# Closing the two seams of a two-block transformer kernel: squares kept apart and added at the end on VectorE, the second panel's matmuls one chunk behind, the third panel split inside the opening

## The reference, cut to what matters

```python
for l in range(DEPTH):                       # first block, DEPTH = 2
    h = rms_norm(x, pre_norm_g[l])
    proj = h @ w_in[l]
    ...
    y = jnp.concatenate([ya, yb], axis=-1) @ w_out[l]
    x = x + rms_norm(y, post_norm_g[l])
...
h = jnp.concatenate([meta, x, ...], axis=1)  # second block
hn = rmsnorm(h, norm_mix[0])
p = hn @ w_in
```

## Time and profile before

| | |
|---|---|
| median of three runs | 2347.67 us (2346.99 to 2349.81) |
| the profiled execution's own time | 2351.86 us |
| its span, first to last instruction | 2350.1 us |
| PE busy | 2241.6 us, 95% of the span |
| DVE, ACT, POOL busy | 1120.9, 971.2, 640.3 us (48%, 41%, 27%) |
| mean granted clock of TensorE | 0.977 of full speed |
| first seam | from about 352 us on |
| second seam | from about 685 us on |

### The profile page before, as it was taken

The page is one execution under the profiler, slowest core; times in us unless marked ns, Lnnn a source line. Parts: engine busy times, 40 slices in busy tenths (PEclk is TensorE's granted clock), DMA queues, the critical chain, the costliest instruction groups (busy, mean ns, idle before and its releaser), DMA issues. The chain is left out here.

```text
span 2350.1 us, 35450 instructions
## 1 busy us (share of the span) xinstructions
PE 2241.6 (95%) x14814; PEld 1988.4 (85%) x14814; DVE 1120.9 (48%) x1665; ACT 971.2 (41%) x1410; POOL 640.3 (27%) x498
## 2 busy tenths in 40 slices
PE   7998999998999999898999999999999989999998
PEld 5886568886579988896799999999898979988987
DVE  2457535657542224795544434444555444443443
ACT  5345643356533325425523313334555533322332
POOL 2112321113222514327223302322333312320321
PEclk9999999999999999997999999999999999999999
DMA  5341023210122211221133333323111113324322
GB/s 187 123 148 47 0 72 100 90 55 5 36 78 73 73 64 41 65 61 70 41 98 90 85 90 103 85 78 98 39 55 37 36 54 91 90 75 114 90 80 73
DMA packets 235215, 175.64 MB, mean 75 GB/s; under 512 B 7732, under 2 KB 230060, under 8 KB 234544
## 3 DMA queue, kind: packets, MB, share of 16 engines
q1 hardware_dynamic: 235056, 173.37, 24.7%
HBM read 171.20 MB, written 10.09 MB: 77 GB/s over the span
## 5 line engine op out<-in xcount | busy, mean ns | idle before, releaser
L331 DVE TENSOR_TENSOR panel_lo<-panel_raw,panel_hi 128x2048 fp32r<-128x2048 f32 (+2 forms) x148 | 325.9, 2202 | 278.1 <-ACT panel_hi L323 278.1
L323 ACT ACTIVATE panel_hi<-panel_raw 128x2048 fp32r<-128x2048 f32 (+2 forms) x151 | 268.4, 1777 | 366.7 <-PE product L429 256.7
L429 PE MATMUL product<-scaled_hi,panel_hi 128*128 128x272 f32 (+2 forms) x1232 | 282.4, 299 | 2.6 <-PEq L485 1.4
L429 PE MATMUL product<-scaled_lo,panel_hi 128*128 128x272 f32 (+2 forms) x1232 | 283.0, 299 | 0.0
L429 PE MATMUL product<-scaled_hi,panel_lo 128*128 128x272 f32 (+2 forms) x1232 | 282.7, 299 | 0.0
L429 PEld LDWEIGHTS product<-scaled_hi,panel_hi 128*128 128x128 f32 x1232 | 196.5, 188 | 11.8 <-issue 3.0
L429 PEld LDWEIGHTS product<-scaled_hi,panel_lo 128*128 128x128 f32 x1232 | 195.4, 188 | 7.4
L429 PEld LDWEIGHTS product<-scaled_lo,panel_hi 128*128 128x128 f32 x1232 | 194.5, 188 | 6.7
L442 PE MATMUL product_banks<-panel_hi,scaled_hi 128*128 128x256 f32 x696 | 195.4, 281 | 3.2 <-DVE panel_lo L331 3.2
L442 PE MATMUL product_banks<-panel_lo,scaled_hi 128*128 128x256 f32 x696 | 195.4, 281 | 0.0
L442 PE MATMUL product_banks<-panel_hi,scaled_lo 128*128 128x256 f32 x696 | 195.3, 281 | 0.0
(11 more groups left out here) (564 smaller groups left out, 5443.0 us busy)
## 6 DMA issues: line engine op xcount, KB each, us to landing
panel_raw<-in_w_in_dram SPq DMA_DIRECT2D x26, 1024.0 KB, 5.4
panel_raw<-in_ffn_w_gate_dram SPq DMA_DIRECT2D x44, 512.0 KB, 4.0
panel_raw<-in_ffn_w_up_dram SPq DMA_DIRECT2D x44, 512.0 KB, 5.3
panel_raw<-in_ffn_w_down_dram SPq DMA_DIRECT2D x32, 704.0 KB, 4.7
panel_raw<-in_even_w_in_dram SPq DMA_DIRECT2D x21, 1024.0 KB, 5.2
panel_raw<-in_odd_w_in_dram SPq DMA_DIRECT2D x12, 1024.0 KB, 5.2
panel_raw<-in_w_out_dram SPq DMA_DIRECT2D x8, 1024.0 KB, 6.8
panel_raw<-in_even_w_out_dram SPq DMA_DIRECT2D x8, 768.0 KB, 4.9
```

What stands on the lines that cost most here:

```text
L323: act.activation(c.hi[g % 2][:, 0:used], c.raw[g % 2][:, 0:used], ACT.Copy).then_inc(c.hi_made.sem, 1)
L331: dve.tensor_tensor(c.lo[g % 2][:, 0:used], c.raw[g % 2][:, 0:used], c.hi[g % 2][:, 0:used].bitcast(F32), ALU.subtract).then_inc(c.lo_made ...
L429: done = pe.matmul(banks[b], weight(w, k), a[:, k, u:v], start=(k == 0 and x == 0), stop=(k == chunks - 1 and x == 2))
```

## The change

It applies to both seams and to nothing else.

1. ACT's squares no longer go through two buffers. Chunk k of the squares is written over chunk k of `update.mix`, which is not needed any more once `hT` has been updated. The 16 meta tokens of the second seam, which are not part of `mix`, are squared ahead of it into a small tile (`extra_squares`).
2. POOL adds nothing any more. After the last chunk DVE adds the eight chunks as a tree of three instructions (2048, 1024 and 512 columns), with three small ones for the 16 meta tokens. PE then sums one total; the second matmul for the last square is gone.
3. PE does chunk k of the first panel's tiles together with chunk k - 1 of the second panel's. The sums stand ahead of the second panel's last chunk in the first seam, and behind it in the second seam (where they stood ahead of the tail tile).
4. The third panel is split inside the opening: on ACT after the last square (first seam) or after the roots (second seam), on DVE after the tree.

```diff
@@ led_product_stage
                 for k in range(KD):
                     if update is not None:
                         update.wait(act, k)
                     parts.act_hi(act, k)
                     if update is not None and k:
-                        norm.act_square(act, k - 1)
+                        norm.act_tree_square(act, k - 1)
                 if update is not None:
-                    norm.act_square(act, KD - 1)
+                    norm.act_tree_square(act, KD - 1)
+                    if wide:
+                        panels.hi(act, first + 2)
...
                 norm.act_inverse(act, sums, columns)
+                if update is not None and not wide:
+                    panels.hi(act, first + 2)
                 act.wait_ge(c.rstd_ready.sem, c.rstd_ready.at(norm.roots))
                 for g in range(first, first + n_panels):
...
-                    if first < g < last_split:
+                    if split_ahead <= g < last_split:
                         panels.hi(act, g + 1)
...
-                dve.wait_ge(c.rstd_ready.sem, c.rstd_ready.at(1))
+                if update is not None:
+                    norm.dve_tree(dve)
+                    panels.lo(dve, first + 2)
+                dve.wait_ge(c.rstd_ready.sem, c.rstd_ready.at(norm.roots))
...
-                if not summed:
-                    for k in range(norm.adds):
+                if not summed and update is None:
+                    for k in range(KD):
                         norm.pool_add(pool, k)
...
+                    in_first = panels.tiles_before(first + 1) - tile_0
+                    head, behind = ([at for at in opening if (at < in_first) == early] for early in (True, False))
+                    for k in range(KD + 1):
+                        if k < KD:
+                            parts.wait(pe, k)
+                            for at in head:
+                                done = chunk(at, k)
+                                if k == KD - 1:
+                                    done.then_inc(c.product_ready.sem, 1)
+                        if k == KD:
+                            if in_first - 1 not in head:
+                                whole_tile(in_first - 1)
+                            if wide:
                                 norm.pe_sums(pe, sums, columns)
+                        if k:
+                            for at in behind:
+                                done = chunk(at, k - 1)
+                                if k == KD:
+                                    done.then_inc(c.product_ready.sem, 1)
+                    if not wide:
+                        norm.pe_sums(pe, sums, columns)
@@ Rstd
+    def act_tree_square(self, act, k):
+        act.activation(self.tree[:, k, :], self.src(k)[:, self.extra:self.tokens], ACT.Square).then_inc(self.c.squared.sem, 1)
+
+    def dve_tree(self, dve):
...
+        each = 2 if extra else 1
+        dve.wait_ge(c.squared.sem, c.squared.at(KD + each - 1))
+        for n, half in enumerate((4, 2, 1)):
+            if n:
+                dve.wait_ge(c.paired.sem, c.paired.at(each * n))
+            a, b = self.tree[:, 0:half, :], self.tree[:, half:2 * half, :]
+            out = a if half > 1 else self.total[:, extra:self.tokens].rearrange("p (k n) -> p k n", k=1)
+            dve.tensor_tensor(out, a, b, ALU.add).then_inc(c.paired.sem, 1)
```

More of the change, by code:

```diff
@@ L234, in open_core @@
     c.x_added = count("x_added")
+    c.paired = count("paired")
     c.inner_made = count("inner_made")
@@ L621, in led_product_stage @@
                     spread=wide if spread is None else spread, side=None if held is None else "right", summed=summed, held=held,
-                    last_on_pe=wide and update is not None)
+                    tree=update.mix if update is not None else None)
         parts = Parts(c, stage if held is None else held, src, tokens, gain, room=whole, side=None if held is None else "right")
@@ L630, in led_product_stage @@
         sums, columns = (free[:, 0:tokens], free[:, 1016:1024]) if own else (psum[SUMS][:, 0, :], psum[COLUMNS][:, 0, 504:512])
+        split_ahead = first + (1 if update is None else 2)
         opening = () if update is None else (0, 1, 2, 3, 4, 5) if wide else (0, 1, 2, 3, 5, 6)
@@ L670, in _ @@
                     panels.hi(act, first)
+                if update is not None:
+                    norm.act_extra(act)
                 for k in range(KD):
@@ L3599, in __init__ @@
     def __init__(self, c, stage, src, tokens, squares=None, total=None, whole=False, columns=True, spread=True, last_on_pe=False,
-                 shape=lambda square: square, side=None, summed=False, held=None):
-        self.summed = summed
+                 shape=lambda square: square, side=None, summed=False, held=None, tree=None):
+        self.summed, self.tree = summed, tree
+        self.extra = tokens - SEQ if tree is not None else 0
+        if tree is not None:
+            squares, total = [], tree[:, 0, :] if total is None else total
+            self.extra_squares = c.sb("extra_squares", [P, KD, self.extra], into=stage) if self.extra else None
         self.c, self.src, self.tokens, self.last_on_pe, self.shape, self.columns = c, src, tokens, last_on_pe, shape, columns
@@ L3605, in __init__ @@
         self.adds = KD - 1 if last_on_pe else KD
-        self.staged = columns and last_on_pe
+        self.staged = tree is not None and spread is not False
         self.roots = 2 if self.staged else 1
-        self.squares = squares or [c.sb(f"squares{j}", [P, tokens], into=stage)[:] for j in range(2)]
+        self.squares = squares if squares is not None else [c.sb(f"squares{j}", [P, tokens], into=stage)[:] for j in range(2)]
         self.total = c.sb("square_total", [P, self.tiles * P if whole else tokens], into=stage)[:] if total is None else total
@@ L3632, in pe_sums @@
         for n, (square, start, stop) in enumerate(parts):
-            if n == 0:
+            if self.tree is not None:
+                pe.wait_ge(c.paired.sem, c.paired.at(6 if self.extra else 3))
+            elif n == 0:
                 pe.wait_ge(c.sum_added.sem, c.sum_added.at(0 if self.summed else self.adds))
@@ L3666, in close @@
         c = self.c
-        squares = () if self.summed else ((c.squared, KD), (c.sum_added, self.adds))
+        if self.tree is not None:
+            squares = ((c.squared, KD + (1 if self.extra else 0)), (c.paired, 6 if self.extra else 3))
+        else:
+            squares = () if self.summed else ((c.squared, KD), (c.sum_added, self.adds))
         for counter, n in (*squares, (c.sums_ready, self.roots), (c.root_made, self.roots), (c.rstd_ready, self.roots)):
```

21 lines of the change are left out of this document (10 added, 11 removed).

## The result

The kernel after took 2330.49 us (median of four runs, 2327.90 to 2331.72) against 2347.33 of before (four runs): ratio 0.9923, interval 0.9909 to 0.9936, or 16.8 us less. The forecast was 2335.9, the range 2332.5 to 2340.5. The sign and both seams came as forecast; 5 us more went than the sum had. A second series of the same kernel, further down, took 2335.99. Two single runs further down, 7602.7 us of before and 2476.35 of the kernel with the third panel late, lie far from all others of their kernels and are left out.

The account below looks back on a forecast made before the run. PE, busy 95% of 2350.1 us, was taken as the bound, with waits and slow stretches in both seams. Gains of 8.1 and 3.7 us, 11.8 in all, off the median 2347.67 gave 2335.9 us, range 2332.5 to 2340.5.

Parts of the forecast that it names:

- the sum: Both seams together: 8.1 us off the first and 3.7 off the second, 11.8 us in all, kept to the end.
- POOL slows DVE, and without it the period is 2.15: First seam: without POOL's additions, DVE's addition to `hT` returns from 1.79 to 0.68 us and its chunk period to 2.15.
- The rival that held POOL innocent: POOL is not what slows DVE: period stays near 3.25 us in the first seam, time 2343 us; chance 0.05.
- Tree 4.3, squares over `mix` at their old cost, sums 1.75: First seam: DVE's three additions take 4.3 us, ACT's squares cost as before, PE's sums halve from 3.49 to 1.75 us.
- The third panel is ready at 380.5; 6.5 and 1.56 in the first seam: First seam: PE goes on at 380.5 instead of 387.03, saving 6.5 us; full clock in tile 6 saves another 1.56.
- the 8.1: First seam's whole gain in us: 6.5 from PE going on earlier and 1.56 from tile 6 at full clock.
- Second seam 3.7, with one wait of 0.5 for the root: Second seam: 4.2 us of PE's idling go, a new 0.5 wait for the root comes, so 3.7 us are gained.
- Waits of half a microsecond don't cost the clock: Both openings: PE's short waits, 0.6 us at 356.7 and brief ones at 380.3 and 711.9, leave the clock full.
- the rival in which such waits cost the clock: Short PE waits in the openings lower the clock, costing 3.2 to 6.4 us; time 2339 to 2342 us; chance 0.10.
- the last of the sum: Stage behind the second seam: the 11.8 us gain is kept, since PE is busy 126.00 of 126 us in 724 to 850.

Follow-up runs that it names:

- the kernel with the third panel late: The kernel after, with the third panel split where before splits it, behind the take of the first panel's tiles, in both seams: 2335.11 us, ratio 0.9940.
- the second profile of before: The unchanged kernel before, run and profiled once more: 2349.09 us, with 0.118 us per matmul throughout the second seam's stage.
- the kernel with one pace: The kernel after, with an unused 192-byte tile ahead of the second seam's scaled tiles, giving distance 0 between weights and panels: 2336.99 us.
- the better version: The kernel after, with unused tiles of 128 and 192 bytes putting all row tiles' weights at distance 64 from the panels: 2327.37 us, ratio 0.9909.
- after once more: The unchanged kernel after, run again beside the others on this chip: 2335.99 us, ratio 0.9939.
- PE alone: Whole computation left out; PE runs the stage's matmul patterns at many addresses, then after pauses: 0.1133 to 0.120 us per matmul of 256 columns at single distances.

## Why the prediction was right, and where it was not

The measured time lies below the range: both seams came about as summed, and what follows them did not.

- *POOL slows DVE, and without it the period is 2.15.* Right: additions of 0.68 in after, 1.53 with POOL's work put back. The rival that held POOL innocent is out.
- *Tree 4.3, squares over `mix` at their old cost, sums 1.75.* Right (4.28; 1.67 from 377.00 to the row tiles' chunk at 378.67).
- *The third panel is ready at 380.5; 6.5 and 1.56 in the first seam.* Right: 6.6 and 1.5. Without its early split 5.5 of the 8.1 are lost.
- *Second seam 3.7, with one wait of 0.5 for the root.* Right at the pace that the sum used (3.9); 4.8 in the first profile, where the opening was at 0.1133 too. It was luck that the one profile of before had the full clock in its opening from 692 on; in the second profile of before, and in the kernel with the first seam alone, tile 7 came 26.8 us after the first matmul and not 24.65.
- *Waits of half a microsecond don't cost the clock.* Right in after: 1.00 in its windows, and the rival in which such waits cost the clock did not come. The ground against it was weaker than it read, though: that the waits of 0.6 and 0.9 in the second seam left the clock at 1.00 holds for that one profile. Behind waits of 0.4 to 0.9 in the same opening the clock was 0.68 in the second profile of before and 0.65 in the kernel with the first seam alone.
- **The step that failed** is the last of the sum: that the gain is kept because PE is busy 126.00 of 126 us in 724 to 850, "so nothing else sets the pace there". A full window says that PE waits for nobody, not that its pace is fixed. 126/1072 = 0.1175 stood in the earlier trace rows and was taken for a constant, as 0.355 for three matmuls was in the opening. A term was missing that is 0 in one execution and some 6 us in another (4.45 ns each on the 1344 matmuls of 256 columns from the opening to the stage's end), by the tiles' distance and by how PE starts behind the root's wait, a wait that the change itself put there. Without it the forecast of 2335.9 holds about: an estimate from the kernel with one pace, 2336.99 less 1344 times 2.2 ns, is 2334.0 on a chip where before took 2347.99. That is 14.0 less and the sum had 11.8, which the ratio's interval takes in. That the second series came to 2335.99 is in part luck, as one of its four runs took 2325.89. That all four runs of the first series had the fast pace is argued from their times: one of them has a profile.

What stays open: which property of a start decides. Waits of 0.38, 0.42 and 0.45 at distance 192 gave slow, fast and slow, and 0.25 gave both; the moments in the stream were not taken apart further. Nor does the ten of twelve carry over to the kernel. Behind the root's wait of 0.45, at distance 64, the stage was fast in three profiles (after, the third panel late, the better version) and slow in three (after once more, the second seam alone, POOL's additions back); at 192, the addresses of before, it was fast in the one there is. So whether the new distance or the new wait made the first series fast is not shown.

## What to carry to other kernels

When a tile is added or dropped, every tile allocated behind it moves, and a matmul's pace can move with it: compare start-to-start times, not busy shares, of stages that the change does not touch. Choose the distance between the weights' and the moving tiles' addresses on purpose, for the widths in use, since 256 and 512 columns don't want the same one (below), and keep chunk strides at multiples of 256 bytes so that it holds for all chunks (256 and 272 columns in turn took 0.1200 to 0.1233 us by distance at a stride of 2304 bytes in PE alone, and 0.1217 to 0.1225 at 2112). A distance with a fast pace may still start at the slow one. Where the runs of a kernel spread wider than those of its neighbour, look for a stage with two paces before reading a gain from one profile.

## What the runs showed of the hardware

The start-to-start time of matmuls of 256 columns (fp32r) at the full clock depends on the distance between weights and moving operand by its rest of 256 bytes: 0.1133, 0.1178, 0.1186 and 0.120 us at 64, 192, 128 and 0; of 512 columns, 0.233, 0.229, 0.232 and 0.227 (at 128 and 0 one group each). At 64 and 192 both of the first two paces lasted, for 48 matmuls in PE alone and for the whole stage in the kernels. A pace outlasted a change of address from 64 to 192 in the one case in which PE went on without a stop; after each of the other changes in that run the pace was that of the new distance. The Trainium skill ("TensorE: Matmul & The Clock Gate", section "Step-by-step: what each phase is for") says that weights and moving operand come through two independent read ports, and that loading the next weights takes no read bandwidth from the running matmul. PE alone does not agree: up to 6% of the pace (0.1133 to 0.120) hangs on where the two lie to each other. What between them costs the time is not shown.
